# Selecting the rows of four experts with 256-wide one-hot matmuls, and two spare weight units, in a three-mixture model

## The chip, the cores and the metric

The kernel runs on one core of one Trainium2 chip. The metric is device microseconds (us) of one execution of the whole program; several executions are taken, and their median counts. One execution was recorded by the hardware profiler.

## What is computed

A three-layer transformer forward pass over 512 tokens of width 1024, all in float32. Each layer is a mixer followed by a mixture of experts. Only the mixture matters here:

```python
g_idx = argmax(x @ w_group + b_group)              # one of 4 groups
top_v, top_i = top_k(expert logits of that group, 2)
gate = g_p * softmax(top_v)
expert_id = g_idx * 8 + top_i                      # 2 of 32 experts per token
# for every block of rows that went to expert e:
h = silu(xb @ w_gate[e]) * (xb @ w_up[e])
y = h @ w_down[e]
out[token] += y * weight
```

Layers 0 and 1 have inner width 512 (6 MiB of weights per expert), layer 2 has 256 (3 MiB per expert). All 32 experts of each layer are computed, so 192 + 192 + 96 MiB of weights are read once each.

## The kernel before, in words

**Units and ring.** SyncE (SP) streams all weights through a ring of 12 buffers of 1 MiB (`ring`, `UNITS = 12`). Unit u may be loaded when `units_used` has reached u - 11, so SP's DMA queue holds at most 12 units ahead of TensorE. An expert of layers 0 and 1 is six units: gate and up of the first half of the 1024 inputs, gate and up of the second half, two of down. An expert of layer 2 is three units.

**Slots.** Every expert has 64 row slots (`BLK`). VectorE builds a one-hot matrix `sel` (`select`, L1622) from `pos`; TensorE multiplies the normalized tokens `hn` by it (`turn_rows`, L833, the matmul is at L839), which at once selects the rows and turns them, so that the result can be the stationary operand of the expert's matmuls. One call of `turn_rows` makes half of the 1024 inputs for a pair of experts: 16 matmuls, each 128x128 stationary and 128 columns moving, into one bank of `XT`; VectorE copies the bank to `xgT` (`copy_rows`, L1633).

**Layers 0 and 1.** `over_blocks` runs four experts written out and then a loop of four experts. `expert` (L844) does, on TensorE: 16 matmuls of gate and 16 of up (L854, 64 stationary columns each, gate and up side by side in the array), then 12 of the 16 matmuls of `turn_rows` for the next pair (`ahead(range(3))`), then waits for `hg`, which ScalarE (silu, L1227) and VectorE (L1706) make, turns `hg` (L830, L831), runs the last 4 matmuls of `turn_rows` (`ahead(range(3, 4))`), waits for VectorE's copy `hT` (L1709), and does the down product (L881). Two calls make a pair, one per expert; `turn_rows` runs in every expert, the last included.

**Layer 2.** `slot` (L951 on) does gate and up of the next expert (`gate_up2`, L927), turns `hg`, calls `ahead2` for a half of the next pair, and does the down product (L967). Pairs 1 to 3 are selected by `turn_rows`; for pairs 4 to 15 GpSimd gathers the rows of the pair from memory (`x_rows`, L1967, 512 KiB each), and TensorE only transposes them (4 transposes at L944 per half).

**GpSimd.** After every pair it scatters 128 result rows to `y_rows` (L1995). When all are stored, SP reads them back and VectorE combines them.

**Spare room.** `hT` (4096 words per partition) holds the turned tokens for the router and is not read after the router's fourth product until the next stage.

Of the kernel before, what the change touches and what calls it, by code (L numbers as in the profile page):

```python
# [4 lines left out]
D = 1024  # L5
S = 512
P = 128
T = S // P
K = D // P
# [5 lines left out]
TURN = 4  # L15
UNITS = 12
# [16 lines left out]
def weight_plan(w):  # L33
# [24 lines left out]
    units += [None] * (E * 6)  # L58
# [5 lines left out]
    units += [None] * (E * 6)  # L64
# [12 lines left out]
def program(nc, t):  # L77
# [17 lines left out]
    slot_token = [nc.dram_tensor(f"slot_token{l}", (rows_, 1), f32, kind="Internal").ap() for l in range(3)]  # L95
    x_rows = nc.dram_tensor("x_rows", (2 * S, D), f32, kind="Internal").ap()

    with ExitStack() as c:
# [39 lines left out]
        rows_zeroed, x_stored = sem("rows_zeroed"), sem("x_stored")  # L138
        xg_loaded = [sem(f"xg_loaded{i}") for i in range(2)]
# [28 lines left out]
        class Steps:  # L168
# [14 lines left out]
            def at_mixture(self, l):  # L183


                self.n0, self.x0, self.sel0 = E * l, (E + 2) * l, (E // 2 + 1) * l
                self.store0 = 16 * (E // 4) * l
# [114 lines left out]
        def over_slots(eng, slot):  # L302


            for s in range(2 * TURN):
                slot(s // TURN, s % TURN)
            with eng.Fori(2, E // TURN - 1) as i:
                for s in range(TURN):
                    slot(i, s)
            for s in range(TURN):  # L310
                slot(E // TURN - 1, s)

# [4 lines left out]
        def over_blocks(eng, body):  # L317


            for s in range(TURN):  # L320
                body(0, s)
            with eng.Fori(1, E // TURN) as i:
                for s in range(TURN):
                    body(i, s)

        sel = [wk(512 * i, 512).rearrange("p (t n) -> p t n", t=T) for i in range(2)]
        xgT = [wk(1024 + 1024 * i, 1024).rearrange("p (k n) -> p k n", k=K) for i in range(2)]
# [40 lines left out]
        xg = [wk(9216 + 2048 * i, D) for i in range(2)]  # L370
# [79 lines left out]
        def _(sp):  # L450
# [20 lines left out]
            def mixture(l):  # L471
                m = moe[l]

                def body(i, s):
                    for q, src in enumerate(expert_units(m, l, TURN * i + s)):
                        u = m.base + m.upb * s + q
                        sp.wait_ge(units_used, u - UNITS + 1 + TURN * m.upb * i)
                        sp.dma_start(ring[u % UNITS][:, :], src).then_inc(unit_loaded[u % UNITS], 16)
# [7 lines left out]
                def slot(i, s):  # L486

                    gate, up, down = (a.rearrange("e (p k) n -> e p k n", p=P) for a in expert_weights)
                    if not last_slot(i, s):
# [1628 lines left out]
```

## Time and profile before

| what | us |
|---|---|
| median of three executions | 2167.49 (2164.78 to 2170.81) |
| the profiled execution, its own time | 2171.3 |
| its span, first to last instruction | 2169.2 |
| TensorE busy (as modelled) | 2003.0 |
| VectorE busy | 675.6 |
| ScalarE busy | 404.9 |
| GpSimd busy | 118.6 |
| mean granted TensorE clock | 0.969 of full |

The profile is a page of totals, and a trace that can be asked by time, by line and by engine. Times in the trace are from the start of the span. PE is TensorE, DVE is VectorE, ACT is ScalarE, POOL is GpSimd, SP is SyncE. A float32 matmul is two MATMUL instructions in the trace. Matmul ends are modelled, so the distance between starts is read rather than the duration; a row of the timeline merges consecutive instructions of one line.

### The profile page before, as it was taken

The numbers are of one execution on the slowest core, as the hardware profiler recorded it, in microseconds if no ns is written. First come the engines' busy times: TensorE is split into PE (matmuls) and PEld (weight loads), VectorE is DVE, ScalarE is ACT, GpSimd is POOL, SyncE is SP. The second block draws the span as 40 slices with busy tenths as digits, with TensorE's granted clock in tenths as the row PEclk, the third lists the DMA queues.
The fourth block names the chain that finished last, engine by engine and source line by source line (L and its number), as shares of the span: only waits on it lengthen the run. The fifth ranks groups of instructions, "written<-read, shape, count | busy, mean of one in ns | idle before, by whom it ended". The sixth has DMA issues, their size and how long they took to land.

```text
span 2169.2 us, 25934 instructions
## 1 busy us (share of the span) xinstructions
PE 2003.0 (92%) x10197; PEld 1076.1 (50%) x10197; DVE 675.6 (31%) x1571; ACT 404.9 (19%) x873; POOL 118.6 (5%) x141
## 2 busy tenths in 40 slices
PE   8999989999999998799999999999599989999873
PEld 4444446545545454645544545545444445665442
DVE  0154547211111111635311111111637223532123
ACT  1133432111111111111111111111233222112112
POOL 0000000100000000000100000000100001021100
PEclk9999999999999999899999999999798989999997
DMA  9511102999999999712799999999721111599995
GB/s 317 165 39 39 39 23 98 355 419 421 421 420 420 421 421 363 268 63 94 271 419 420 421 421 421 421 420 402 269 84 39 39 39 30 188 344 414 420 420 238
DMA packets 121892, 593.39 MB, mean 274 GB/s; under 512 B 15857, under 2 KB 41345, under 8 KB 58847
## 3 DMA queue, kind: packets, MB, share of 16 engines
q1 hardware_dynamic: 108495, 565.96, 65.8%
q0 software_dynamic: 13328, 26.49, 3.7%
q8 instruction: 45, 0.74, 0.1%
q14 instruction: 24, 0.20, 0.0%
HBM read 572.95 MB, written 35.44 MB: 280 GB/s over the span
## 4 chain that ended last, share of the span: by engine, by line
PE 82%; DMA 11%; DVE 4%; ACT 2%; issue 1%; SPq 0%; ACTq 0%; DVEq 0%; POOLq 0%
PE bank L854 19%; PE bank L839 12%; PE bank L597 10%; PE bank L881 10%; DMA ring<-in_w_up_dram 5%; PE bank L739 4%; PE bank L609 4%; DMA ring<-in_moe_w_up_dram 4%; PE bank L927 3%; PE bank L583 3%; PE bank L967 1%; PE bank L1096 1%; PE bank L693 1%; PE bank L830 1%; PE bank L666 1%
## 5 line engine op out<-in xcount | busy, mean ns | idle before, releaser
L854 PE MATMUL bank<-ring,work 128*64 128x512 f32 x2048 | 451.4, 592 | 1.8 <-DMA ring<-in_moe_w_up_dram 1.4
L854 PEld LDWEIGHTS bank<-ring,work 128*64 128x64 f32 x2048 | 146.7, 137 | 293.2 <-issue 292.5
L839 PEld LDWEIGHTS bank<-work 128*128 128x128 f32 x2240 | 260.1, 191 | 57.0 <-issue 52.3
L839 PE MATMUL bank<-work 128*128 128x128 f32 x2240 | 285.6, 281 | 0.0
L1706 DVE TENSOR_TENSOR work<-work,bank 64x512 f32<-64x512 f32 x64 | 67.8, 1060 | 612.5 <-ACT work L1227 612.5
L597 PE MATMUL bank<-hT,ring 128*128 128x512 f32 x512 | 238.5, 609 | 0.7 <-ACT work L1159 0.7
L881 PE MATMUL bank<-ring,work 128*64 128x512 f32 x1024 | 233.8, 598 | 0.0
L597 PEld LDWEIGHTS bank<-hT,ring 128*128 128x128 f32 x512 | 94.3, 194 | 110.0 <-issue 108.2
L927 PE MATMUL bank<-ring,work 128*64 128x256 f32 x1024 | 116.9, 380 | 25.2 <-DMA ring<-in_w_up_dram 24.8
L1232 ACT ACTIVATE work<-bank 64x512 f32<-64x512 f32 x64 | 37.8, 590 | 484.7 <-PE bank L881 475.6
L881 PEld LDWEIGHTS bank<-ring,work 128*64 128x64 f32 x1024 | 67.6, 136 | 117.5 <-issue 109.8
L927 PEld LDWEIGHTS bank<-ring,work 128*64 128x64 f32 x1024 | 78.9, 137 | 72.8 <-issue 39.3
L1227 ACT ACTIVATE work<-bank 64x512 f32<-64x512 f32 x64 | 37.7, 589 | 355.3 <-PE bank L854 355.3
L1995 POOL DMA_INDIRECT y_rows<-work,y_row x48 | 46.7, 973 | 1043.1 <-ACT work L1233 894.0
L1633 DVE COPY work<-bank 128x512 f32<-128x512 f32 x97 | 67.1, 692 | 73.7 <-PE bank L839 57.6
L609 PE MATMUL bank<-ring,hT 128*128 128x512 f32 x192 | 82.9, 593 | 1.7 <-DMA ring<-in_attn_w_qkv_dram 1.7
L583 PE MATMUL bank<-hT,ring 128*128 128x128 f32 x512 | 63.4, 288 | 5.6 <-ACT hT L1135 5.6
L583 PEld LDWEIGHTS bank<-hT,ring 128*128 128x128 f32 x512 | 61.9, 203 | 7.6 <-ACT hT L1135 7.6
L967 PE MATMUL bank<-ring,work 128*64 128x512 f32 x256 | 62.0, 604 | 3.6 <-issue 1.9
L1709 DVE COPY work<-bank 128x256 f32<-128x256 f32 x64 | 27.2, 425 | 111.5 <-PE bank L831 111.5
L609 PEld LDWEIGHTS bank<-ring,hT 128*128 128x128 f32 x192 | 36.3, 190 | 47.8 <-issue 47.0
L1737 DVE COPY work<-bank 128x128 f32<-128x128 f32 x32 | 9.3, 292 | 160.7 <-PE bank L831 158.3
(293 smaller groups left out, 1875.6 us busy)
## 6 DMA issues: line engine op xcount, KB each, us to landing
ring<-in_moe_w_gate_dram SPq DMA_DIRECT2D x128, 1024.0 KB, 17.4
ring<-in_moe_w_up_dram SPq DMA_DIRECT2D x128, 1024.0 KB, 19.6
ring<-in_moe_w_down_dram SPq DMA_DIRECT2D x128, 1024.0 KB, 17.8
ring<-in_w_gate_dram SPq DMA_DIRECT2D x32, 1024.0 KB, 21.1
ring<-in_w_up_dram SPq DMA_DIRECT2D x32, 1024.0 KB, 22.4
ring<-in_w_down_dram SPq DMA_DIRECT2D x32, 1024.0 KB, 21.7
ring<-in_attn_w_qkv_dram SPq DMA_DIRECT2D x12, 1024.0 KB, 13.4
work<-y_rows SPq DMA_DIRECT2D x12, 1024.0 KB, 8.7
```

The source lines that it names most:

```text
L583: mm = pe.matmul(bank[2 * i + half][:, P * tt:P * tt + P], v[:, k, P * half:P * half + P], hT[:, k, P * tt:P * tt + P], start=(k == 0), st ...
L597: mm = pe.matmul(banks[:, :], v[:, k, 128 * half:128 * half + 128], hT[:, k, :], start=(k == 0), stop=(k == K - 1))
L609: mm = pe.matmul(banks[tt][:, :], operand[:, 4 * kk + k, P * tt:P * tt + P], v[:, k, :], start=(kk + k == 0), stop=(kk + k == 4))
L739: mm = pe.matmul(bk[:, :], operand(k, tt), v[:, k % 4, :], start=(k == (0 if l else 4)), stop=(k == last))
L839: mm = pe.matmul(XT[half][:, P * k:P * k + width], src[:, tt, c0:c0 + P], sel[buf][:, tt, 0:width], start=(tt == 0), stop=(tt == T - 1))
L854: mm = pe.matmul(GU[BLK * a:BLK * a + BLK, :], xT_[:, 4 * kk + k, :], v[:, k, :], start=(kk + k == 0), stop=(kk + k == 4))
L881: mm = pe.matmul(DN[BLK * n:BLK * n + BLK, :], hT_[:, 2 * kk + k, :], v[:, k, 512 * n:512 * n + 512], start=(kk + k == 0), stop=(2 * kk + ...
L927: mm = pe.matmul(GU2[s % 2][BLK * a:BLK * a + BLK, 0:F], xgT[pair % 2][:, k, BLK * of_pair:BLK * of_pair + BLK], v[a][:, k, :], start=(k = ...
L967: mm = pe.matmul(DN[BLK * n:BLK * n + BLK, :], hgT[:, P * k // 2:P * k // 2 + BLK], v[:, k, 512 * n:512 * n + 512], start=(k == 0), stop=( ...
L1633: dve.tensor_copy(xgT[buf][:, 4 * half:4 * half + 4, 0:width], XT[half][:, :].rearrange("p (k n) -> p k n", k=4)[:, :, 0:width])\
L1706: dve.tensor_tensor(dealt(hg[:, 0:F], F // P), as_dealt(sg[:, 0:F], F // P), as_dealt(GU[BLK:P, 0:F], F // P), ALU.mult).then_inc(b.hg, 1)
L1995: pool.indirect_dma_start(out=y_rows, out_offset=bass.IndirectOffsetOnAxis(ap=y_row[:, q:q + 1], axis=0), in_=ysb[q % 2], in_offset=None, ...
```

## The change

- The one-hot matrix is made for four experts at a time (`QUAD` = 256 columns). `turn_group(i, s)` makes two of the eight blocks of inputs for the whole next group: 8 matmuls, 256 columns moving. One call stands in each expert, after the gate and up product; in the first expert of layers 0 and 1 it stands after the turn of `hg`, and 32 narrow matmuls for the second pair (`turn_second_pair`) stand before it.
- Nothing stands between the turn of `hg` and the down product any more in the other experts of layers 0 and 1, and no selection is done in the last group.
- `over_quads` takes the place of both loop helpers: one group written out, a loop of three rounds over two groups, one group written out.
- Layer 2: `turn_second_pair` stands between gate and up of experts 0 and 1; slot 0 makes two parts of group 1; groups 1, 2, 4 and 6 are selected by one-hot matmuls, groups 3, 5 and 7 are gathered (two gathers of a pair each, issued when results of pairs 0 to 1, 0 to 5 and 0 to 9 are stored).
- The first two units of the last expert of each layer go to `hT` (`spare`, `SPARE = 2`) instead of the ring. SP issues them behind the unit loads of expert 1 (behind those of slot 2 in layer 2), when the router's last product is done. All later units move two places forward in the ring.

The core of the diff:

```diff
+QUAD = TURN * BLK
+SPARE = 2
-    units += [None] * (E * 6)
+    units += [None] * (E * 6 - SPARE)
...
-        def over_slots(eng, slot):
-        def over_blocks(eng, body):
+        def over_quads(eng, body):
             for s in range(TURN):
+                body(0, s, 0)
+            with eng.Fori(0, (E // TURN - 2) // 2) as r:
+                for b in (1, 2):
+                    for s in range(TURN):
+                        body(2 * r + b, s, b % 2)
+            for s in range(TURN):
+                body(E // TURN - 1, s, (E // TURN - 1) % 2)
...
# SP
+                def load_spare():
+                    sp.wait_ge(routing.logits, T * (l + 1))
+                    sources = expert_units(m, l, E - 1)
+                    for a in range(SPARE):
+                        src = next(sources)
+                        dst = spare[a] if l < 2 else spare[a].rearrange("p a n -> p (a n)").rearrange("p (k n) -> p k n", k=K)
+                        sp.dma_start(dst, src).then_inc(spare_loaded, 16)
...
# TensorE
+                def turn_second_pair():
+                    pe.wait_ge(main.sel, main.sel0 + 1)
+                    for half in range(2):
+                        turn_rows(main, half, P, P)
+
+                def turn_group(i, s, par):
+                    gathered = l == 2 and par == 0 and (type(i) is not int or i > 0)
+                    if s == 0 and not gathered:
+                        pe.wait_ge(main.sel, main.sel0 + 2 + i)
+                    pe.wait_ge(main.xT, main.x0 + 3 + s + TURN * i)
+                    if gathered:
+                        if s == 0:
+                            pe.wait_ge(rows_gathered, 16 * i)
+                        for k in range(2):
+                            for half in range(2):
+                                c0 = P * (2 * s + k)
+                                mm = pe.transpose(XT[s % 2][:, QUAD * k + P * half:QUAD * k + P * half + P],
+                                                  pair_rows[half][:, c0:c0 + P], ident)
+                        mm.then_inc(main.xt, 1)
+                        return
+                    for k in range(2):
+                        for tt in range(T):
+                            c0 = P * (2 * s + k)
+                            mm = pe.matmul(XT[s % 2][:, QUAD * k:QUAD * k + QUAD], src[:, tt, c0:c0 + P],
+                                           sel[1 - par][:, tt, :], start=(tt == 0), stop=(tt == T - 1))
+                    mm.then_inc(main.xt, 1)
...
                     if ahead is not None:
-                        ahead(range(3))
+                        ahead(0)
                     pe.wait_ge(b.hg, b.n0 + j + 1)
                     for k in range(half_f):
                         mm = turn_block(k, HT[:, BLK * k:BLK * k + BLK], hg[:, P * k:P * k + P], ident[BLK:P, BLK:P])
                     mm.then_inc(b.ht, 1)
                     if ahead is not None:
-                        ahead(range(3, 4))
+                        ahead(1)
                     pe.wait_ge(b.hT, b.n0 + j + 1)
...
+                    def ahead(part):
+                        if first_one and part == 0:
+                            turn_second_pair()
+                        elif part == first_one and not (type(i) is int and i == E // TURN - 1):
+                            turn_group(i, s, par)
...
+                def ahead2(i, s, par):
+                    if type(i) is int and TURN * i + s == 0:
+                        turn_group(i, 0, par)
+                    if type(i) is not int or TURN * i + s < E - TURN - 1:
+                        turn_group(i + 1 if s == TURN - 1 else i, (s + 1) % TURN, (par + (s + 1) // TURN) % 2)
...
# VectorE
-                select(1, 2)
+                select(0, 2, P, 2)
+                if l < 2:
+                    select(1, TURN, 0, TURN)
...
+                    def ahead():
+                        if type(i) is int and j == 0:
+                            copy_second_pair()
+                        copy_group(i, s, par)
-                    if s % 2:
-                        select(pair % 2, j + 3)
+                    if s == 2 and not (type(i) is int and i == E // TURN - 1):
+                        select(par, j + 6, 0, TURN)
...
# GpSimd, layer 2
-                    if l == 2 and 6 <= q + 4 < E // 2:
-                        gather_rows(q + 4)
+                    if l == 2 and q in (2, 6, 10):
+                        gather_quad({2: 3, 6: 5, 10: 7}[q])
```

`copy_group` is one copy of a bank (128x512) to `xg`; `select(buf, e, lo, count)` issues one VectorE compare of 256 columns per expert.

## Rows read from the trace of the kernel before

**Rows 1.** The chain that ended last, by engine.

```profile
PE 82%; DMA 11%; DVE 4%; ACT 2%; issue 1%; SPq 0%; ACTq 0%; DVEq 0%; POOLq 0%
```

**Rows 2.** Windows: length, busy PE, PEld, DVE, ACT, POOL, clock, DMA share, GB/s.

```profile
384.00:400.00 16.00, 16.00 (x94) 8.21 (x91) 5.58 (x18) 2.30 (x4) 7.32 (x8) 1.00 0.86 283
370.00:378.00 8.00, 6.29 (x38) 5.58 (x38) 4.62 (x21) 1.28 (x2) 0.00 (x0) 0.79 0.00 0
437.00:840.00 403.00, 403.00 (x2293) 203.55 (x2291) 68.65 (x107) 47.87 (x81) 13.54 (x14) 1.00 1.01 420
2010.00:2120.00 110.00, 88.33 (x636) 51.58 (x634) 21.56 (x41) 20.65 (x40) 12.00 (x12) 1.00 1.01 419
```

**Rows 3.** Timeline of TensorE, one expert in the steady part of layer 0.

```profile
796.72 7.04 PE L854 MATMUL bank<-ring,work 128*64 128x512 f32 x32
803.69 2.94 PE L839 MATMUL bank<-work 128*128 128x128 f32 x24
806.56 0.43 PE L830 MATMUL bank<-con,work 64*128 64x64 f32 x2
...
808.20 3.65 PE L881 MATMUL bank<-ring,work 128*64 128x512 f32 x16
811.68 7.04 PE L854 MATMUL bank<-ring,work 128*64 128x512 f32 x32
```

**Rows 4.** Timeline of TensorE: first matmuls of layer 0, its last expert.

```profile
377.38 7.09 PE L854 MATMUL bank<-ring,work 128*64 128x512 f32 x32
...
845.80 3.65 PE L854 MATMUL bank<-ring,work 128*64 128x512 f32 x16 [0.58 <-DMA ring<-in_moe_w_up_dram]
...
853.90 3.65 PE L881 MATMUL bank<-ring,work 128*64 128x512 f32 x16
```

**Rows 5.** The chain in order of time: layer 1's first and last matmuls.

```profile
1039.59 7.09 PE bank L854 x32
...
1516.96 3.61 PE bank L881 x16
```

**Rows 6.** Timeline of VectorE in layer 0: the product hg, both copies.

```profile
385.20 1.05 DVE L1706 TENSOR_TENSOR work<-work,bank 64x512 f32<-64x512 f32 x1 [3.30 <-ACT work L1227]
...
807.22 0.43 DVE L1709 COPY work<-bank 128x256 f32<-128x256 f32 x1 [1.73 <-PE bank L831]
808.31 0.69 DVE L1633 COPY work<-bank 128x512 f32<-128x512 f32 x1 [0.66 <-PE bank L839]
```

**Rows 7.** The chain in order of time: narrow selection, layer 2's gate and up.

```profile
1917.19 3.77 PE bank L839 x32
...
1956.68 3.45 PE bank L927 x32
1963.02 3.45 PE bank L927 x32
```

**Rows 8.** Timeline of TensorE in layer 2.

```profile
1886.70 3.67 PE L927 MATMUL bank<-ring,work 128*64 128x256 f32 x32 [0.32 <-ACT work L1217]
...
1913.15 3.62 PE L927 MATMUL bank<-ring,work 128*64 128x256 f32 x32
1922.66 3.62 PE L927 MATMUL bank<-ring,work 128*64 128x256 f32 x32
...
2126.79 0.43 PE L830 MATMUL bank<-con,work 64*128 64x64 f32 x2
...
2127.67 1.94 PE L967 MATMUL bank<-ring,work 128*64 128x512 f32 x8 [0.38 <-DVE work L1737]
...
2136.98 0.43 PE L830 MATMUL bank<-con,work 64*128 64x64 f32 x2
...
2138.39 1.94 PE L967 MATMUL bank<-ring,work 128*64 128x512 f32 x8 [0.92 <-DVE work L1737]
```

**Rows 9.** The chain in order of time: the last result scatter of two layers.

```profile
859.56 3.62 DMA y_rows<-work,y_row
...
2142.33 2.62 DMA y_rows<-work,y_row
```

More of the change, by code:

```diff
@@ L63, in weight_plan @@
     first["moe1"] = len(units)
-    units += [None] * (E * 6)
+    units += [None] * (E * 6 - SPARE)
     for lo in (2056, 2312):
@@ L300, in turn_bank, with gu_in_ring, down_unit, xg @@
             return bank[(2 * tt + kk) % 8]
-        def over_slots(eng, slot):
[L305 to L309, printed above, removed]
-            for s in range(TURN):
-                slot(E // TURN - 1, s)
+        def over_quads(eng, body):
+            for s in range(TURN):
+                body(0, s, 0)
[5 more added lines that the diff above has]
+                body(E // TURN - 1, s, (E // TURN - 1) % 2)
         def last_slot(i, s):
             return type(i) is int and TURN * i + s == E - 1
-        def over_blocks(eng, body):
[L320 to L329, printed above, removed]
+        def gu_in_ring(i, s):
+            return type(i) is not int or TURN * i + s < E - 2
+        def down_unit(i, s):
+            return 3 * s + (0 if last_slot(i, s) else 4 if gu_in_ring(i, s) else 2)
+        sel = [wk(lo, T * QUAD).rearrange("p (t n) -> p t n", t=T) for lo in (0, 4352)]
+        def xg(par, k, n=1):
+            lo = 1024 + QUAD * k if par else 9216 + 2048 * (k // 4) + QUAD * (k % 4)
+            return wk(lo, QUAD * n).rearrange("p (k n) -> p k n", k=n)
+        pair_rows = [wk(lo, D) for lo in (4352, 16384)]
+        spare = [hT[:, 4 * a:4 * a + 4, :] for a in range(SPARE)]
         pos = wk(7572, T * (E + 4)).rearrange("p (t n) -> p t n", t=T)
@@ L484, in load2, with slot @@
                     sp.dma_start(ring[u % UNITS][:, :], src).then_inc(unit_loaded[u % UNITS], 16)
-                def slot(i, s):
+                def slot(i, s, par):
                     gate, up, down = (a.rearrange("e (p k) n -> e p k n", p=P) for a in expert_weights)
-                    if not last_slot(i, s):
+                    if gu_in_ring(i, s):
                         load2(i, 3 * s + 2, gate[TURN * i + s + 1])
                         load2(i, 3 * s + 3, up[TURN * i + s + 1])
-                    load2(i, 3 * s + (2 if last_slot(i, s) else 4), down[TURN * i + s])
+                    load2(i, down_unit(i, s), down[TURN * i + s])
+                    if type(i) is int and TURN * i + s == 2:
+                        load_spare()
                 if l < 2:
-                    over_blocks(sp, body)
+                    over_quads(sp, body)
                 else:
@@ L831, in turn_block, with turn_rows @@
                     return pe.transpose(out, rows, eye)
-                def turn_rows(b, buf, half, width, ks=range(4)):
-                    for k in ks:
+                def turn_rows(b, half, lo, width):
+                    for k in range(4):
                         for tt in range(T):
@@ L853, in expert @@
                                     v = unit(2 * kk + a).rearrange("p (k n) -> p k n", k=4)
-                                    mm = pe.matmul(GU[BLK * a:BLK * a + BLK, :], xT_[:, 4 * kk + k, :], v[:, k, :],
+                                    mm = pe.matmul(GU[BLK * a:BLK * a + BLK, :], xT_(4 * kk + k), v[:, k, :],
                                                    start=(kk + k == 0), stop=(kk + k == 4))
-                            mm.then_inc(b.used, 2)
+                            if kk or not in_spare:
+                                mm.then_inc(b.used, 2)
                     else:
@@ L917, in unit2, with gate_up2 @@
                     return ring[u % UNITS][:, :]
-                def gate_up2(i, s):
-                    pair, of_pair = s // 2, s % 2
-                    pe.wait_ge(main.xT, main.x0 + TURN * i + 2 * pair + 2)
-                    v0 = 0 if type(i) is int and i + s == 0 else 3 * s - 1
-                    v = [unit2(i, v0 + a).rearrange("p (k n) -> p k n", k=K) for a in range(2)]
+                def gate_up2(i, s, par):
+                    b, quad = BLK * (s % TURN), (par + s // TURN) % 2
+                    in_ring = gu_in_ring(i, s - 1)
+                    pe.wait_ge(main.xT, main.x0 + (2 if type(i) is int and TURN * i + s < 2 else 4) +
+                               TURN * (s // TURN) + TURN * i)
+                    v0 = 0 if type(i) is int and TURN * i + s == 0 else 3 * s - 1
+                    if in_ring:
+                        v = [unit2(i, v0 + a).rearrange("p (k n) -> p k n", k=K) for a in range(2)]
+                    else:
+                        pe.wait_ge(spare_loaded, 16 * SPARE * (l + 1))
+                        v = [spare[a].rearrange("p k n -> p (k n)").rearrange("p (k n) -> p k n", k=K) for a in range(2)]
                     for k in range(K):
```

201 lines of the change are left out of this document (104 added, 97 removed).

## The prediction

> **What bounds the kernel now.** I read the chain that ended last first: 82% of it is TensorE, 11% DMA [rows 1]. That is an average, so the windows come next. In layer 0's steady part TensorE has work in all 403 of 403 us, and DMA has share 1.01 at 420 GB/s: both are full. In layer 2's later part DMA is again at 1.01, but TensorE has work in only 88 of 110 us: there DMA bounds. Between 370 and 378 us, before the first expert, DMA is idle; from 384 to 400 its share is 0.86, so about 2.3 us are idle [rows 2].
>
> Which of the two sets layer 0's end is told by the timeline. Experts start 811.68 - 796.72 = 14.96 us apart [rows 3]. The layer runs from 377.38 to 853.90 + 3.65 = 857.55, so 480.2 us; 32 x 14.96 = 478.7. TensorE waits for DMA once, 0.58 us, in the last expert [rows 4]. DMA's own price: at 420 GB/s a 1 MiB unit takes 2.50 us, six units with half a result scatter (0.26 MB) 15.6 us. So DMA loses 0.6 us per expert on TensorE and has just used up the ring's lead at the end. Layer 1 takes 1516.96 + 3.61 - 1039.59 = 481.0 us [rows 5], some 2 us of it waits. Layers 0 and 1 are a tie: what frees only one of the two brings nearly nothing.
>
> **The change in layers 0 and 1, part by part.**
> *Narrow to wide.* 16 narrow matmuls take 3.77 us [rows 7]. A 256-column part is 8 matmuls. A price for 256 columns is in layer 2's gate and up: 16 matmuls in 3.45 us, two side by side in the array, so 8 pairs in 3.45 [rows 7]. Its bounds: above, twice the narrow price, 8 x 2 x 3.77/16 = 3.77; below, the 3.45 itself, since half of the 512-column price, 6.97 us for 8 pairs in layer 0, is 3.49 [rows 3]. I take 3.45, the row of the same width, and 0.05 for the change of line: 3.50.
> *The lost filler.* Before, from the end of gate and up to the down product pass 808.20 - 803.69 = 4.51 us: 12 narrow matmuls, the turn of hg (from 806.56), and 4 narrow ones [rows 3]. Those 4 hid VectorE's copy, which starts 0.66 us after the turn began and takes 0.43 [rows 3, 6]. Now nothing hides it: 0.66 + 0.43, and 0.06 for the signal back, make 1.15. Layer 2's last slots, where nothing is selected, show such a hole: 2127.67 - 2126.79 = 0.88 with a turn and a copy half as large, 0.38 of it idle [rows 8]. New: 3.50 + 1.15 = 4.65, against 4.51. So the wide selection saves 0.5 us per expert of matmuls and the hole takes it all: +0.14, cadence 15.10, for experts 1 to 27: +3.8. Bounds for the 1.15: 0.55 (the copy hidden after all; what the 4.51 leaves for the turn) and 1.41, the longest of layer 2, in its last slot (2138.39 - 2136.98) [rows 8].
> *First expert.* 7.0 (gate and up), 32 narrow 7.54, then the turn; VectorE copies hgT (0.66 + 0.43), then the second pair's first bank (0.69), and only then may TensorE start the first part: 1.84. Part 3.50, down 3.48: 23.4 instead of 15.0, +8.4. The second bank's copy and the later ones lie beside TensorE.
> *Last four experts.* No selection. The turn waits for hg, which the selection covered: gate and up ended at 377.38 + 7.0 = 384.4, VectorE's product came at 385.20 and takes 1.05 [rows 4, 6], so 1.9. 7.0 + 1.9 + 1.15 + 3.48 = 13.5, -1.45 each, -5.8.
> Sum for layer 0: 23.4 + 27 x 15.10 + 4 x 13.5 + 0.2 (slot table, tail) = 485.3, +5.1; layer 1 +4.3.
> *Does DMA allow this?* The first of the four units freed by expert 0's gate and up is issued near 381; at 2.5 us each, with the small traffic of the slot tables, they keep DMA busy to about 391.5; its down units come free at 399 instead of 391, so about 7.5 us are idle instead of 2.3: DMA is 5.2 us later. The two spare units are loaded while DMA was idle (after the router's last product, before the first expert [rows 2]) and take 5.0 us out of the stream. The last up unit, landed at 845.7 before, lands at 846 again. TensorE wants it at 377.4 + 23.4 + 407.7 + 3 x 13.5 + 3.5 = 852.6. It no longer waits; the spare units buy nothing here that could be used.
> *Covered, at nothing.* VectorE's compares: some 1.5 us more before the index chain, which ends before expert 0's hg, where VectorE had 3.30 us of idle [rows 6]; 1.5 us per group later, behind the copies, while TensorE does the down product and the next 7 us of gate and up. Were the cover gone, 1.5 us per group. load_spare waits for the router on SP; behind it are only loads that wait for expert 0. GpSimd is unchanged.
> *After the layer.* The last result scatter took 3.62 us with weights still streaming, 2.62 without [rows 9]. The stream now ends before it: -1.0 in each layer.
>
> **Layer 2.** Before: 1886.70 to 2138.39 + 1.94 = 2140.3, 253.6 us. Slots with 16 narrow matmuls take 1922.66 - 1913.15 = 9.51 [rows 8]; with a gathered half 6.34 [rows 7]. New one-hot slot: 9.51 - 3.77 + 3.45 = 9.19. There are 16 one-hot parts, two in slot 0, 12 gathered parts (again 4 transposes: 6.34), 4 slots with none (about 6.2, since 0.88 us pass where the transposes covered it). Gate and up 3.6, second pair 7.54, slot 0 12.7, 14 x 9.19 = 128.7, 12 x 6.34 = 76.1, 24.8, and the last slot 3.4 (2136.98 to 2140.3 [rows 8]): 257.0 with the slot table, +3.4. DMA loses 6 gathers (1.25 us each at 420 GB/s) and 2 units: its stream is 12.5 us shorter. It needs 7.5 to 8.1 us per slot's three units, less than 9.19: the ring is full when a gathered group begins, loses three units in its four slots and wins them back. So TensorE bounds here too. The gathers stand behind result scatters in GpSimd's queue. By the sum, slot 3 ends near 1939, the first two gathers are issued by 1945, and slot 7 wants them at 1966; several times the 3.6 us of a scatter [rows 9] is covered. Each gather is issued before GpSimd waits for the next results, so the scatters, and ScalarE's reuse of their buffers, are not held up. On SP, unit 11 now waits behind the spare loads for the router; slot 4 wants it near 1930.
>
> **Sum:** +5.1 + 4.3 - 2.0 + 3.4 = **+10.8 us**. Against the profiled execution's 2171.3 that is 2182.1; this execution was 3.8 above the median, so I forecast 2167.5 + 10.8 = **2178.3 us**.
>
> **One rule against my wide price.** Matmuls of 512 columns follow at 6.97/8 = 0.87 us per pair in gate and up, narrow ones at 0.236: 3.7 times for four times the columns [rows 3, 7]. The Trainium skill, TensorE: Matmul & The Clock Gate, section Back-to-back issue gap, says that a stream of loads and matmuls runs at 81 ns per matmul for 128 columns and 131 for 512, 1.6 times; an estimate from it between the two makes a 256-column matmul 1.2 times a narrow one. By that rule a part would cost 2.3 us and the kernel would be DMA-bound; the trace disagrees.
>
> **Rivals.**
> B, *same*: the hole after the turn costs almost nothing, so that TensorE's cadence is under 14.86. That is the point of decision: the 6.4 us between 846 and 852.6, over 27 experts, is 0.24 each. Then DMA ends both layers 1 us earlier; with the scatters -4.0, layer 2 +3.4: 2167. For it: modelled ends hide small gaps. Against: layer 2 shows the 0.38 us of idle.
> C, *faster*: a wide matmul costs much less than two narrow ones. Mechanism: weight loads, one per matmul, set the pace of narrow ones and streaming does not add up. 1.2 us less per part. Layers 0 and 1 go by DMA (-4.0), layer 2 too, -12.5: 2151. This is the time by the skill's rule as well. Against: the 512-column rows.
> D, *much slower*: a wide matmul costs two narrow ones, 3.77 + 0.05: +0.3 for 54 + 16 parts, +21: 2199. Against: 256 columns at 3.45 in layer 2, but with 64 columns to load, not 128.
>
> **Numbers.** A 0.60, B 0.20, C 0.10, D 0.10. A measurement of this kernel tells 0.3%, 6.5 us, from no change. A's own spread (2170 to 2188: hole and first expert by a few tenths each, on 56 experts) reaches over that bound a little: slower 0.66, same 0.24, faster 0.10. The range 2166 to 2192 holds A and B, and part of the way to D.
>
> **What would show it.** Right: experts of layer 0 about 15.1 us apart, the down product 1.15 us after the turn, first expert 23 us, last four 13.5, no DMA waits of TensorE in any layer, layer 2 at 257 us with one-hot slots of 9.2. Wrong: wide parts not 3.5 us, DMA waits that return before the last expert, or a TensorE wait for a gather.

## The result, and the profile after

The changed kernel takes **2197.94 us** (median of four, 2195.10 to 2199.37) against 2167.28 before (four runs beside it, 2164.78 to 2170.81): ratio 1.0139, interval 1.0121 to 1.0156, so slower by 1.4%. I had forecast 2178.3 with a range up to 2192. The sign and the bounding engine were right, the size was not: +10.8 forecast, +30.7 measured.

First the page of after, two lines of it: the queue on which instructions are fetched (45 packets and 0.74 MB before: the code is longer), and the chain by engine, which answers to [rows 1].

```profile
q8 instruction: 52, 0.85, 0.2%
...
PE 89%; DVE 5%; ACT 2%; DMA 2%; issue 1%; SPq 0%; DVEq 0%; POOLq 0%; ACTq 0%
```

DMA has left the chain (11% to 2%), and VectorE's share grew from 4% to 5%. The windows of after answer to [rows 2] (columns as there):

```profile
382.00:402.00 20.00, 18.79 (x121) 12.89 (x119) 8.38 (x25) 2.51 (x4) 8.32 (x9) 1.00 0.56 212
437.00:800.00 363.00, 350.60 (x1646) 162.21 (x1644) 58.35 (x96) 42.13 (x72) 11.58 (x12) 1.00 1.01 420
1470.00:1530.00 60.00, 52.66 (x236) 19.48 (x234) 6.92 (x11) 7.09 (x12) 1.93 (x2) 0.94 1.01 405
2010.00:2120.00 110.00, 110.00 (x739) 69.20 (x737) 23.40 (x47) 21.47 (x41) 10.86 (x11) 1.00 1.01 419
```

In the first expert DMA's share is down to 0.56 (before 0.89 in the same window, 382 to 402): its units are freed later. In layer 0's steady part TensorE now has gaps (350.60 of 363), in layer 2 it has none left (110 of 110, before 88.33). DMA still shows 1.01: it always has work, which doesn't make it the bound. The time that TensorE waited tells it apart; the list of its waits from 380 to 880 us is complete with three lines, none of them DMA (columns: waiting line, releaser: us in total, times, longest):

```profile
PE bank L933 <- DVE work L1787: 16.0, 31, 0.5
PE bank L852 <- DVE work L1784: 7.0, 4, 1.8
PE bank L891 <- DVE work L1697: 1.2, 1, 1.2
```

The first line is the idle part of the forecast hole, once in each of 31 experts (in the first one the part fills it). TensorE's timeline shows a steady expert of layer 0, to be laid beside [rows 3], and then the last expert but two:

```profile
433.30 7.04 PE L905 MATMUL bank<-ring,work 128*64 128x512 f32 x32
440.27 3.72 PE L891 MATMUL bank<-work 128*128 128x256 f32 x16
443.92 0.43 PE L852 MATMUL bank<-con,work 64*128 64x64 f32 x2
...
445.06 3.65 PE L933 MATMUL bank<-ring,work 128*64 128x512 f32 x16 [0.52 <-DVE work L1787]
448.54 1.03 PE L905 MATMUL bank<-ring,work 128*64 128x512 f32 x4
...
827.66 7.04 PE L905 MATMUL bank<-ring,work 128*64 128x512 f32 x32
836.45 0.43 PE L852 MATMUL bank<-con,work 64*128 64x64 f32 x2 [1.75 <-DVE work L1784]
```

The cadence is 448.54 - 433.30 = 15.24 us: 6.97 + **3.65** + 1.14 + 3.48. The first mixture goes from 379.25 to the end of its last down product (start 864.41, 3.65 long), 488.8 us.

Where the time went, by mixture (first gate and up matmul to the end of the last down product) and by what lies between. All numbers are of the two profiled executions, whose spans differ by 27.0; the one of before was 3.8 us over its median, the one of after 0.2. The differences are of the unrounded times.

| us | before | after | difference | forecast |
|---|---|---|---|---|
| up to layer 0's mixture | 377.4 | 379.2 | +1.9 | 0 |
| mixture 0 | 480.2 | 488.8 | +8.6 | +5.1 |
| between | 182.0 | 184.1 | +2.1 | -1.0 |
| mixture 1 | 481.0 | 492.1 | +11.1 | +4.3 |
| between | 366.2 | 359.8 | -6.4 | -1.0 |
| mixture 2 | 253.6 | 263.4 | +9.7 | +3.4 |
| tail | 28.8 | 28.8 | 0.0 | 0 |

The stretches outside the mixtures sum to -2.5, close to the -2.0, but not for my reason: most of the -6.4 stands where nothing was changed, and in the other runs' profiles that stretch takes anything from 358.9 to 369.8 us. So the missing 17 us are all in the mixtures.

### The profile page after: what moved, and what is told of

It reads as the page before. It is cut to its first block, busy times and chain, and to the rows that moved or that the text cites. A ratio compares the mean times of both kernels' runs of the same rounds, so it can differ in the third digit from the quotient of the medians.

```text
span 2196.2 us, 23921 instructions
## 1 busy us (share of the span) xinstructions
PE 2010.5 (92%) x9269; PEld 1045.4 (48%) x9269; DVE 670.8 (31%) x1584; ACT 404.9 (18%) x873; POOL 111.7 (5%) x135
## 4 chain that ended last, share of the span: by engine, by line
PE 89%; DVE 5%; ACT 2%; DMA 2%; issue 1%; SPq 0%; DVEq 0%; POOLq 0%; ACTq 0%
PE bank L905 20%; PE bank L891 12%; PE bank L933 11%; PE bank L619 10%; PE bank L992 5%; PE bank L761 4%; PE bank L631 4%; PE bank L605 3%; PE bank L1026 3%; PE bank L852 2%; PE bank L1155 1%; PE bank L715 1%; DVE work L1787 1%; PE bank L688 1%; PE bank L1116 1%
## 5 line engine op out<-in xcount | busy, mean ns | idle before, releaser
L905 PEld LDWEIGHTS bank<-ring,work 128*64 128x64 f32 x2016 | 144.3, 137 | 286.8 <-issue 285.9
L891 PE MATMUL bank<-work 128*128 128x256 f32 x1168 | 271.3, 385 | 2.4 <-DVE work L1697 2.4
L891 PEld LDWEIGHTS bank<-work 128*128 128x128 f32 x1168 | 216.0, 190 | 74.0 <-issue 46.4
L933 PEld LDWEIGHTS bank<-ring,work 128*64 128x64 f32 x1024 | 68.6, 138 | 153.2 <-issue 112.6
L992 PEld LDWEIGHTS bank<-ring,work 128*64 128x64 f32 x992 | 72.5, 137 | 46.9 <-issue 16.6
L631 PE MATMUL bank<-ring,hT 128*128 128x512 f32 x192 | 84.3, 601 | 1.9 <-DMA ring<-in_attn_w_qkv_dram 1.9
L1709 DVE COPY work<-bank 128x512 f32<-128x512 f32 x85 | 58.2, 684 | 63.8 <-PE bank L891 60.2
L761 PE MATMUL bank<-ring,hT 128*128 128x512 f32 x128 | 57.5, 597 | 0.8 <-ACT hT L1194 0.8
## 6 DMA issues: line engine op xcount, KB each, us to landing
ring<-in_moe_w_down_dram SPq DMA_DIRECT2D x128, 1024.0 KB, 10.5
ring<-in_w_gate_dram SPq DMA_DIRECT2D x31, 1024.0 KB, 10.5
```

Source lines behind the costliest of these rows:

```text
L631: mm = pe.matmul(banks[tt][:, :], operand[:, 4 * kk + k, P * tt:P * tt + P], v[:, k, :], start=(kk + k == 0), stop=(kk + k == 4))
L761: mm = pe.matmul(bk[:, :], operand(k, tt), v[:, k % 4, :], start=(k == (0 if l else 4)), stop=(k == last))
L891: mm = pe.matmul(XT[s % 2][:, QUAD * k:QUAD * k + QUAD], src[:, tt, c0:c0 + P], sel[1 - par][:, tt, :], start=(tt == 0), stop=(tt == T - 1))
L905: mm = pe.matmul(GU[BLK * a:BLK * a + BLK, :], xT_(4 * kk + k), v[:, k, :], start=(kk + k == 0), stop=(kk + k == 4))
L933: mm = pe.matmul(DN[BLK * n:BLK * n + BLK, :], hT_[:, 2 * kk + k, :], v[:, k, 512 * n:512 * n + 512], start=(kk + k == 0), stop=(2 * kk + ...
L992: mm = pe.matmul(GU2[s % 2][BLK * a:BLK * a + BLK, 0:F], xg(quad, k)[:, 0, b:b + BLK], v[a][:, k, :], start=(k == 0), stop=(k == K - 1))
```

## The experiments

Three chips were used for the runs below (3 for e1, e2, e4 and e5; 4 for e0, e8, e9, p1 and p2; 7 for e6, e10 and e11); each comparison is with runs of the kernel before on the same chip. The mixtures of all runs, each from its profiled execution:

| run | ratio to before (95%) | mixture 0 | 1 | 2 |
|---|---|---|---|---|
| e0_again, the changed kernel | 1.0191 (1.0156 to 1.0225) | 494.6 | 499.3 | 263.1 |
| e1_split | 1.0107 (1.0066 to 1.0148) | 487.1 | 485.4 | 263.4 |
| e2_narrow | 1.0258 (1.0219 to 1.0297) | 499.1 | 499.7 | 266.6 |
| e4_short (selects too little) | 1.0113 (1.0070 to 1.0156) | 483.1 | 487.1 | 263.1 |
| e5_short_nospare (the same) | 1.0097 (1.0058 to 1.0135) | 488.3 | 485.5 | 263.1 |
| e6_nospare | 1.0202 (1.0184 to 1.0220) | 497.5 | 497.4 | 263.1 |
| e9_lastfill | 1.0183 (1.0156 to 1.0211) | 495.2 | 494.5 | 263.1 |
| e8_spread | 1.0040 (1.0018 to 1.0061) | 480.8 | 478.6 | 263.1 |
| e10_guard | 1.0177 (1.0162 to 1.0192) | 500.5 | 497.4 | 260.1 |
| e11_repaired | 1.0050 (1.0033 to 1.0067) | 478.5 | 481.6 | 259.9 |
| p1_spare_before | 0.9967 (0.9948 to 0.9986) | 476.6 | 478.7 | 253.1 |
| p2_guard_before | 0.9983 (0.9969 to 0.9997) | 477.1 | 479.0 | 253.7 |

**What a wide matmul costs, and what the hole costs.** Two kernels that differ from the changed one in the parts alone. e1_split puts half of each part behind the turn:

```diff
-                        elif part == first_one and not (type(i) is int and i == E // TURN - 1):
-                            turn_group(i, s, par)
+                        elif not (type(i) is int and i == E // TURN - 1):
+                            turn_group(i, s, par, range(2) if first_one else range(part, part + 1))
```

> Layers 0 and 1: the first 4 of the 8 wide matmuls before the turn of hg, the other 4 behind it, as the narrow ones stood in the kernel before; everything else as changed. Theory 1 (the unfilled hole after the turn sets TensorE's pace, and TensorE the end): the down product follows within 0.1 us of its filler, experts come 14.65 us apart instead of 15.24, DMA (15.6 per expert) catches up and ends layers 0 and 1 some 10 us earlier each: about 2178 us. Theory 2 (the hole only shows in modelled times, something else sets the pace): no more than 3 us off 2198.

e2_narrow makes each wide matmul two narrow ones, in the same place:

```diff
-                            mm = pe.matmul(XT[s % 2][:, QUAD * k:QUAD * k + QUAD], ... sel[1 - par][:, tt, :], ...)
+                        for q in range(2):
+                            mm = pe.matmul(XT[s % 2][:, QUAD * k + P * q:QUAD * k + P * q + P], ... sel[1 - par][:, tt, P * q:P * q + P], ...)
```

> Every wide matmul of 256 columns as two of 128 columns at the same place, stationary loaded twice; in all layers. Theory 1 (a wide matmul costs what two narrow ones cost): 3.65 us for a part stays within 0.05, total within 3 us of 2198. Theory 2 (widening saved weight loads): a part takes 3.77 or more, 71 parts, 8 us or more slower, 2206 or above.

TensorE's timeline of e1_split:

```profile
452.89 7.04 PE L907 MATMUL bank<-ring,work 128*64 128x512 f32 x32
459.85 1.99 PE L892 MATMUL bank<-work 128*128 128x256 f32 x8
461.78 0.43 PE L852 MATMUL bank<-con,work 64*128 64x64 f32 x2
...
462.33 1.99 PE L892 MATMUL bank<-work 128*128 128x256 f32 x8
464.25 3.65 PE L935 MATMUL bank<-ring,work 128*64 128x512 f32 x16
467.73 1.03 PE L907 MATMUL bank<-ring,work 128*64 128x512 f32 x4
```

and of e2_narrow:

```profile
452.67 7.04 PE L906 MATMUL bank<-ring,work 128*64 128x512 f32 x32
459.63 3.84 PE L892 MATMUL bank<-work 128*128 128x128 f32 x32
463.40 0.43 PE L852 MATMUL bank<-con,work 64*128 64x64 f32 x2
...
464.54 3.65 PE L934 MATMUL bank<-ring,work 128*64 128x512 f32 x16 [0.52 <-DVE work L1788]
468.02 7.04 PE L906 MATMUL bank<-ring,work 128*64 128x512 f32 x32
```

The hole is real and is nothing but the copy: with four wide matmuls behind the turn the idle 0.52 us vanishes and the cadence is 14.84 (forecast 14.65), 0.40 less, of which 27 experts make 10.8 us. Against e0_again (the changed kernel once more, on another chip; below), mixture 0 is 7.5 and mixture 1 is 13.8 shorter; the rest of both numbers is the first expert and slow down products in the last four, which differ from run to run. The ratio falls from e0_again's 1.0191 to 1.0107, 18 us against the 20 of the expectation, but e0_again stands higher than the 2198 that I had started from. DMA did not catch up, as I had expected it to: TensorE waits for it nowhere in mixture 0 and once, 0.6 us, in mixture 1.

In e2_narrow two narrow matmuls in place of each wide one cost 3.77 per part against 3.65: wide matmuls save 3%, not the 7% I had given them. Over 73 parts (28, 28 and 17 in the three layers) that is 8.8 us, as in the second theory of the expectation, and the mixtures together are 8.4 us longer than e0_again's; the medians of the two differ by more (ratio 1.0258 against 1.0191, two chips), and the profiled execution of e2_narrow was 8 us under its median, so some 6 us stay unexplained. By the Trainium skill (TensorE: Matmul & The Clock Gate, Back-to-back issue gap), an estimate between its figures for 128 and 512 columns makes a matmul of 256 columns cost 1.2 narrow ones. This trace disagrees: 3.65/8 = 0.456 us for 256 columns against 3.77/16 = 0.236 for 128, 1.9 times.

**Where the floor of DMA lies.** In e4_short the parts of layers 0 and 1 take 2 matmuls instead of 8 (what is left out stands in the expectation); e5 and e6 take the spare units away, from e4_short and from the changed kernel:

```diff
+                    few = 1 if l < 2 else T
...
-                        for tt in range(T):
+                        for tt in range(few):
...
-SPARE = 2
+SPARE = 0
```

> In layers 0 and 1 the parts for groups 1 to 7 select from the first 128 tokens alone (2 wide matmuls instead of 8), so that TensorE needs about 12.5 us per expert. It shows what DMA alone allows. Theory 1 (TensorE bounds the changed kernel in layers 0 and 1): DMA waits come back, experts go at 15.6 us in the end, layers 0 and 1 end some 10 us earlier each, 2178. Theory 2 (DMA, or its idle time in the first expert, bounds them already): no change, 2198.

> As the run with the short selection, and without the two spare units (12 units of ring only). Where DMA sets the end, two units are worth 2 x 2.5 us per layer: 10 us slower than with them (2188) if the spare units do what they are for in layers 0 and 1, and nothing in layer 2. Rival: the spare loads hold up others and bring nothing: the same time as with them.

> The changed kernel without the two spare units (all 192 units of a layer go through the ring). My forecast said that they buy nothing in layers 0 and 1: the last up unit lands near 846 + 5.0 = 851 us, TensorE wants it at 852.6. With the measured cadence of 15.24 TensorE wants it later still, near 856, so the theory is: mixtures of layers 0 and 1 as in the changed kernel (488.8 and 492 us on the first chip, 494.6 and 499.3 on this one), no DMA wait over 0.5 us, layer 2 unchanged, total within 0.3 per cent of the changed kernel. Rival: the spare units are what removes the DMA waits; without them the last four experts of each layer wait, 5 us per layer, total 5 to 10 us more than the changed kernel.

TensorE's timeline of e4_short:

```profile
561.29 3.65 PE L906 MATMUL bank<-ring,work 128*64 128x512 f32 x16 [1.33 <-DMA ring<-in_moe_w_up_dram]
...
571.89 3.65 PE L906 MATMUL bank<-ring,work 128*64 128x512 f32 x16 [0.41 <-DMA ring<-in_moe_w_up_dram]
576.89 3.65 PE L906 MATMUL bank<-ring,work 128*64 128x512 f32 x16 [1.34 <-DMA ring<-in_moe_w_up_dram]
```

With TensorE relieved, experts 3 to 8 come 13.4 us apart, on the ring's lead, and then TensorE waits for DMA, 31 times and 32.4 us in mixture 0. From there on experts mostly come 576.89 - 561.29 = 15.60 and 14.96 us apart in turn (the next up product starts at 591.85), on average over experts 9 to 29 15.34 in mixture 0 and 15.36 in mixture 1; in e5 it is 15.28 and 15.37. That is DMA's own price of an expert, and it is less than the 15.6 that the prediction made from 420 GB/s. So with nearly free parts DMA takes over after some eight experts, and with the first expert as long as the change makes it, mixtures 0 and 1 stay at 483 and 487: a cadence under 15.3 lasts only while the ring's lead lasts. The changed kernel's 15.24 is just under it. In e6_nospare TensorE waits for no DMA either, and its ratio is that of e0_again within the intervals: in the changed kernel the spare units buy nothing, as forecast. In e5 mixture 0 is 5.2 longer than in e4 and mixture 1 is 1.5 shorter, and the medians are equal (2192.2 and 2192.3): the 10 us of the expectation did not come, and what the spare units are worth in mixture 0 stays inconclusive.

**The ends of layers 0 and 1.** Unexpected in the first profile was this stretch of after (TensorE's timeline, layer 1's last group):

```profile
1495.99 0.43 PE L852 MATMUL bank<-con,work 64*128 64x64 f32 x2 [1.75 <-DVE work L1784]
...
1497.13 5.35 PE L933 MATMUL bank<-ring,work 128*64 128x512 f32 x16 [0.52 <-DVE work L1787]
1502.31 7.04 PE L905 MATMUL bank<-ring,work 128*64 128x512 f32 x32
...
1512.24 5.22 PE L933 MATMUL bank<-ring,work 128*64 128x512 f32 x16 [0.52 <-DVE work L1787]
```

A down product takes 5.3 us instead of 3.65 after TensorE idled 1.75 and 0.52 us, and the window around it has a granted clock of 0.94: part of it ran at the lower level, 1.2 GHz. The unedited kernel was run again, and one with four useless wide matmuls before the turn in the last four experts (e9_lastfill):

```diff
+                        elif part == 0:
+                            for tt in range(T):
+                                pe.matmul(XT[0][:, 0:QUAD], src[:, tt, 0:P], sel[0][:, tt, :], start=True, stop=True)
```

> The changed kernel again, unedited, beside the next three, so that they are compared on one chip, and to see whether its first expert and its last four look the same in another execution. Theory 1 (TensorE's idle in the last four experts, 2.3 us of 13.4, lets its clock fall now and then): between 0 and 3 of the down products of experts 28 to 31 in each of layers 0 and 1 take 5.3 us instead of 3.65. Theory 2 (the long down products of layer 1 wait for late weights): they appear in layer 1 alone.

> The changed kernel with 4 useless wide matmuls before the turn of hg in experts 28 to 31 of layers 0 and 1, where TensorE otherwise waits 1.75 us for hg; results go to a free bank. Theory 1 (clock): no down product of 5.3 us is left, the four experts take 13.5 us each, granted clock 1.00 there; total up to 5 us less than the unedited one. Theory 2 (late weights): the long products stay and the total is the same.

TensorE's timeline of e0_again and then of e9_lastfill, layer 1's last group:

```profile
1507.23 5.35 PE L933 MATMUL bank<-ring,work 128*64 128x512 f32 x16 [0.52 <-DVE work L1787]
...
1535.85 6.61 PE L933 MATMUL bank<-ring,work 128*64 128x512 f32 x16 [0.52 <-DVE work L1787]
...
1552.22 5.25 PE L933 MATMUL bank<-ring,work 128*64 128x512 f32 x16 [0.52 <-DVE work L1787]
```

```profile
1503.65 1.99 PE L965 MATMUL bank<-work 128*128 128x256 f32 x8
1505.57 0.43 PE L852 MATMUL bank<-con,work 64*128 64x64 f32 x2
...
1506.71 3.65 PE L933 MATMUL bank<-ring,work 128*64 128x512 f32 x16 [0.52 <-DVE work L1790]
```

The second theory (late weights, layer 1 alone) falls: in e0_again one down product of mixture 0 is long too (4.97 us), beside three in mixture 1, and none of these waited for DMA. In e9_lastfill the useless matmuls take 1.92 us, 0.17 more than the wait that they fill, every down product is back at 3.65, and the granted clock from 1495 to 1550 us is 1.00 (0.91 in e0_again): the idle time set the clock. Mixture 1 is 4.8 shorter for it. Mixture 0 is not, since e0_again had lost only 1.3 us there and the first expert of e9_lastfill happened to be 1.6 longer; the ratio shows no gain that can be told from none.

**The first expert.** e0_again showed a second surprise. TensorE's timeline of e0_again in expert 0, and then VectorE's:

```profile
395.17 0.35 PE L853 MATMUL bank<-con,work 64*128 64x64 f32 x3
398.99 5.07 PE L891 MATMUL bank<-work 128*128 128x256 f32 x16 [3.48 <-DVE work L1697]
403.99 3.65 PE L933 MATMUL bank<-ring,work 128*64 128x512 f32 x16
407.47 2.75 PE L905 MATMUL bank<-ring,work 128*64 128x512 f32 x12
```

```profile
388.37 1.06 DVE L1784 TENSOR_TENSOR work<-work,bank 64x512 f32<-64x512 f32 x1 [2.93 <-ACT work L1286]
397.82 0.42 DVE L1787 COPY work<-bank 128x256 f32<-128x256 f32 x1 [8.39 <-remote]
398.16 1.28 DVE L1697 COPY work<-bank 128x512 f32<-128x512 f32 x2
```

TensorE had turned hg by 395.52, but VectorE's copy started at 397.82, and the profile names no instruction that ended its idle time ("remote"). VectorE itself was not late: the trace's record of the semaphore that TensorE's turn raises has it go up at 397.80, 2.28 us after the turn's modelled end and 0.02 before the copy. In the first profile of the changed kernel it went up 0.01 us after the end, and in the steady part of mixture 0 TensorE's signals come 0.01 to 0.03 us after the ends (profiles of before, after and e0_again). The kernel before has such a late signal too, in the same place, but on the copy of the next pair's first bank (raised at 391.21, 2.23 us after the end of the last narrow matmul):

```profile
391.24 0.69 DVE L1633 COPY work<-bank 128x512 f32<-128x512 f32 x1 [2.40 <-remote]
```

There the copy was for a later expert, and TensorE had the down product and the next gate and up to run meanwhile. In the changed kernel the second pair's selection stands ahead of the copies and the part behind them, so that the wait is on TensorE's path, and the part runs slow (5.07 instead of 3.65: from 398.90 to 404.00 the granted clock is 0.72, so part of it ran at the lower level; 1.00 from 395 to 399 in the first profile). The first expert takes 407.47 - 379.83 = 27.6 us instead of the 23.3 of the first profile. e8_spread is e1_split with the second pair spread over experts 0 and 1 and group 1 over experts 2 and 3:

```diff
+                        if type(i) is int and i == 0:
+                            if s < 2:
...
+                                turn_rows(main, s, P, P, range(3, 4) if part else range(3))
+                            else:
+                                turn_group(i, 2 * (s - 2) + part, par)
```

> Layers 0 and 1: wide parts split around the turn as in the first experiment, and the work of the first expert spread: the second pair's narrow matmuls in experts 0 and 1 (as in the kernel before), the four parts of group 1 in experts 2 and 3, two each. Theory 1 (the first expert's 23 us starve DMA by 5 us and carry a 1.2 to 4.5 us wait for VectorE, so DMA's end is late): first expert 15 us, layers 0 and 1 about 478 to 481 us each instead of 487 and 485 with the split alone; total about 2175. Rival (spreading only moves the same TensorE work): the same as the split alone, 2191.

Mixtures 0 and 1 get another 6.3 and 6.8 us shorter than in e1_split (run on another chip), 6.2 and 5.9 of it in the first four experts, and they now stand at 480.8 and 478.6, level with before and within the forecast 478 to 481; the total, 2181.4, missed the forecast 2175. Against e0_again on the same chip, filling the hole and spreading the first expert's pile of selection are worth 13.7 and 20.7 us in the two mixtures. They are therefore what made layers 0 and 1 slower there. In the first profile, where the signal was not late, TensorE waited only 1.21 us behind the pile; there the +8.6 of mixture 0 is +8.3 up to the first down product, +7.4 over the next 27 experts and -7.0 over the last four.

**Layer 2's useless part.** TensorE's timeline of after near the end of layer 2:

```profile
2135.96 3.62 PE L992 MATMUL bank<-ring,work 128*64 128x256 f32 x32
...
2139.94 3.72 PE L891 MATMUL bank<-work 128*128 128x256 f32 x16
2143.59 1.94 PE L1026 MATMUL bank<-ring,work 128*64 128x512 f32 x8
2145.36 3.62 PE L992 MATMUL bank<-ring,work 128*64 128x256 f32 x32
```

This is slot 27, and it selects for a ninth group that does not exist: slot 27 stands in the loop, where `type(i) is not int` holds and the guard of `ahead2` lets it pass. e10_guard writes groups 5 and 6 of layer 2 out, e11_repaired is e8_spread with the same edit:

```diff
+            alone = 3 if body.__name__ == "slot" else 1
-            with eng.Fori(0, (E // TURN - 2) // 2) as r:
+            with eng.Fori(0, (E // TURN - 1 - alone) // 2) as r:
```

> The changed kernel, but groups 5 and 6 of layer 2 are written out beside group 7 instead of standing in the loop, so that the guard against a ninth group holds and slot 27 selects nothing. Theory: the part in slot 27 (3.72 us, 16 matmuls of line 891) stood on TensorE's path alone: layer 2's mixture 263.2 -> 259.5 us, the whole 3.7 less than the changed kernel (2212.2 on this chip in the run before, 2197.9 on the first). Rival: layer 2 is set by DMA there, the slot then waits for its units: under 1 us gained. Second rival: the longer code costs instruction fetches in layer 2, and 1 to 3 us of the 3.7 come back as remote waits.

> The split parts, the second pair spread over experts 0 and 1, and the guard for slot 27, all in one. Theory: the costs found add up: the split and spread kernel stood at 2181.4 (ratio 1.004), less 3.7 for slot 27: 2177.7, ratio 1.002, so still not faster than the kernel before, because layer 2 is 259.5 against 253.6 and layers 0 and 1 stand within 3 us of before. Rival: the filler was all that was wrong and the wide form with spare units now wins by 3 us or more: ratio under 0.9985.

The timeline of e10_guard, the same slot:

```profile
2148.74 3.62 PE L994 MATMUL bank<-ring,work 128*64 128x256 f32 x32
...
2153.18 1.94 PE L1028 MATMUL bank<-ring,work 128*64 128x512 f32 x8 [0.38 <-DVE work L1824]
2154.94 3.62 PE L994 MATMUL bank<-ring,work 128*64 128x256 f32 x32
```

The slot takes 2154.94 - 2148.74 = 6.20 instead of 9.40 us. Of the 3.7 that were expected 3.2 came, since the hole of 0.38 opened behind the turn, and layer 2 went from 263.1 to 260.1. In the total of e10_guard it can hardly be seen: 1.0177 against 1.0191 on another chip, intervals overlapping. On its own chip e6_nospare, whose layer 2 takes 263.1 us too, stands at 1.0202, 5.3 us more by the medians, with intervals that overlap by little. The mixture 0 of e10_guard was long (500.5) because three of the last four down products ran slow (5.35, 6.58 and 5.24). e11_repaired keeps both gains in its mixtures, but its ratio, 1.0050, is not under e8_spread's 1.0040: by the profile 8 us of it stand ahead of layer 0's mixture (386.1 us against 377.6 to 380.1 in the other edited kernels), in one execution that was the longest of its six. The repaired kernel is in any case slower than before, by 0.3 to 0.7%.

**What in the change could be kept.** The last two experts of layers 0 and 1 selected for a pair that does not exist, in the kernel before. p1_spare_before drops that and adds the two spare units; p2_guard_before drops it alone (both also write the last group out behind the loop):

```diff
+        def pair_ahead(i, s):
+            return not (type(i) is int and TURN * i + s >= E - 2)
...
-                    expert(main, ..., unit, need, ahead)
+                    expert(main, ..., unit, need, ahead if pair_ahead(i, s) else None, late > 0)
```

> The kernel before with only the two spare units added, and the selection for a pair that does not exist left out (experts 30 and 31 of layers 0 and 1). Narrow matmuls, fillers, first expert and the gathers of layer 2 as before. Theory 1 (spare units are worth 5 us per layer where DMA sets the end and TensorE can follow): layers 0 and 1 some 4 us shorter each, layer 2 5 us: about 2154. Rival (spare loads only fill time that DMA had anyway, or the clock falls in the last two experts): 2164 or above.

> The kernel before without the selection for a pair that does not exist in the last two experts of layers 0 and 1, and without spare units: what p1 was, less its two spare units. The run of p1 gave ratio 0.9967, mixtures 476.6, 478.7 and 253.1 us. Theory: the tie of TensorE and DMA in the kernel before means that TensorE's saving at the end is worth nothing without a shorter stream: the last units land when they did (about 845.7 to 850), the last experts wait for DMA, mixtures 480 and 481 as before, ratio 0.999 to 1.001. Rival: the spare units buy nothing, the dropped selection was all of p1's gain: mixtures 477 and 479, ratio 0.997.

p1 is faster than before by 0.33% (0.14 to 0.52), p2 by 0.17% (0.03 to 0.31); they are the only versions that beat the kernel before. Their mixtures 0 and 1 differ by 0.4 us each (unrounded), and their medians by 1.3 (2162.4 and 2163.7); the kernel before, beside them on the same chip, had moved by 5.7 (2172.5 and 2166.8). p1's first theory, 4 to 5 us per layer and 2154, falls: against the profile of before its mixtures are 3.6, 2.3 and 0.5 us shorter. Here too the clock takes part back where nothing is selected: one down product of mixture 1 took 5.16 us in p1, one 5.35 in p2. My theory for p2 falls: without spare units no wait for DMA came back in mixture 0, and of the 3.6 us by which p1's mixture 0 is shorter than that of before (480.2), 3.1 are in p2 too. Whether the spare units bring the rest can't be told from these intervals.

## Why the prediction was wrong in size

What held: the first expert (23.29 us in the first profile, forecast 23.4), the turn to the down product (1.14, forecast 1.15), the last four experts (13.41, forecast 13.5), no DMA wait in any layer, TensorE as the bound of layer 2, and no wait for a gather. Rival B falls with that: the hole does cost its 0.5 us.

DMA's price of an expert, 15.6 us in the prediction, was too high: 15.3 to 15.4 by e4 and e5. It did not enter the sum, which went by TensorE's cadence. The steps that failed, against the mixtures' 17 us:

1. **"I take 3.45, the row of the same width, and 0.05 for the change of line: 3.50."** Measured 3.65. The row of the same width had two matmuls of 64 columns side by side; the other bound, twice the narrow price (3.77), was nearer, and e2_narrow measured it in place. 15.24 - 15.10 = 0.14 over 27 experts is 3.8 us in each of layers 0 and 1; in layer 2 the one-hot slot takes 9.40 (as 2145.36 - 2135.96 above) instead of 9.19, 14 times, 2.9. Together 10.5 of the 17. Rival D named this mechanism, a wide matmul at the price of two narrow ones, and put it at twice the size: +0.3 per part, where +0.15 was measured.
2. **"4 slots with none"** in layer 2. I read the guard as if it held inside the loop; one slot had a part. 3.2 us by e10_guard.
3. **"7.0 + 1.9 + 1.15 + 3.48 = 13.5"** for the last four experts counts TensorE's waits as idle time alone. In layer 1 they also cost clock: 5.35 - 3.65 and 5.22 - 3.65, 3.3 us.

10.5 + 3.2 + 3.3 = 17.0, against 29.5 - 12.8 = 16.7 in the mixtures (measured less forecast). With the forecast's 10.8 and the -0.5 by which the stretches between came out lower (-2.5 for -2.0) this is the spans' 27. The medians differ by 3.6 us more, because the profiled execution of before stood 3.8 over its median and that of after 0.2. The forecast took the 3.8 off the base, but its terms were read from the long execution; the -6.4 in an unchanged stretch says where part of that length was. The scatter's gain of 1.0 was had in layer 1 (2.75 us in the chain at 1546.29, against 3.71 before) and not in layer 0 (3.50 at 870.08, against 3.62 [rows 9]).

Rival D's time, 2199, came out right to 1 us by luck: it had 21 us for wide matmuls alone. Rival C's time was wrong for a reason beyond the price: e4_short, with parts at a third of the cost in layers 0 and 1, has these mixtures at 483.1 and 487.1, not under the 480.2 and 481.0 of before.

The range failed because all three misses were of one sign, and two of them were no spread of a price but terms that the sum did not have.

## What to carry to other kernels

Work that an engine does while it waits is not free to move: before a selection is made wider or moved ahead, list for each wait what fills it now (the 4 matmuls that hid a 0.43 us copy, the down product and the next gate and up that ran beside a late signal), since the 3% that wide matmuls saved was less than what they uncovered. Price an operation by a row with the same shape of both operands, and if there is none, measure that first. And read every guard for both kinds of its loop variable, where a loop body is partly written out.

## What was not expected of the hardware

- A down product behind 1.75 + 0.52 us of idle in 13.4 took 3.65 us in some experts and 5.0 to 6.6 in others, with the granted clock of the 60 us window down to 0.94 in after; filling the first wait with useless matmuls brought all of them to 3.65. Which of the four experts are hit, and how many (none to three in a layer), changed from run to run.
- In the first expert of layers 0 and 1 TensorE's signal for the turned hg went up 2.2 to 3.5 us after the turn's modelled end in all eight later runs with the changed first expert (e0, e1, e2, e4, e5, e6, e9 and e10), on all three chips, and VectorE's copy started 0.02 us after the signal; TensorE then waited 3.4 to 4.7 us for the copies. In the first profile of the changed kernel the signal was on time and it waited 1.21. The kernel before and e8_spread have signals as late in the same stretch, behind which TensorE does not wait; p2_guard_before has none. Whether TensorE's work or only its signal was late, and what spared the first profile, stays open; no run varied it.
- This and the slower matmuls are why the same kernel stood at 1.0139 in the first runs and at 1.0191 in e0_again, as far as one profile of each can say: the first experts are 4.3 and 4.1 us longer, and slow down products cost 1.3 and 3.0 more, 12.7 of the 13.7 by which the spans differ.
- 16 wide float32 matmul instructions take 3.65 us, 32 narrow ones 3.77: from 128 to 256 columns the time goes by columns, and twice the count of instructions costs only 3%.
